# Attention with its steps in pairs, in all four head groups: transposes of two steps, then scores of two steps

## The chip, the cores and the metric

The kernel runs on one core of a Trainium2 chip (trn2). The metric is the device time of one execution in microseconds (us). TensorE (PE) does the matmuls and the transposes, and its weight loads (PEld) are recorded apart from them; VectorE (DVE) and ScalarE (ACT) do the elementwise work, GpSimd (POOL) a few powers and accumulating transfers, SyncE (SP) issues most transfers. Every engine takes its instructions in the order of its program and waits at semaphores.

## What is computed

One layer: a sparse attention mixer and a SwiGLU, each behind an RMS norm, for 512 tokens of width 2048. With 512 tokens each query may see all blocks of keys that lie before it, so the selected and the window branch both become causal attention, with keys and values of their own.

```python
h = rms_norm(x, norm_mix_g)
proj = h @ w_in                                   # 16 heads of queries, 6 x 4 groups of keys and values
o_cmp = softmax(q k_cmp) v_cmp                    # compressed blocks
o_sel = softmax(q k_sel, causal) v_sel            # branch b = 0
o_win = softmax(q k_win, causal) v_win            # branch b = 1
x = x + (g0 * o_cmp + g1 * o_sel + g2 * o_win) @ w_out
h = rms_norm(x, norm_ffn_g)
x = x + (silu(h @ w_gate) * (h @ w_up)) @ w_down
```

## The kernel before

Each engine has its own hand-written program in the kernel; there is no planner. Numbers in float32 are split into a high and a low part, and a product is three matmuls (`mm3`, L1674 is the line of every matmul in the traces): high by high, high by low, low by high. The weights come in units of 128 x 1024 elements: ScalarE copies the high part (`split`, L616), VectorE subtracts to get the low part (L1019).

**Groups and steps.** The attention runs in four groups of four heads. A group has 32 steps: for each head h, two branches b, and in each four tiles of queries, t = 0 to 3. Step i has t = i % 4, and its scores span t + 1 tiles of 128 keys. What is done for a step:

- TensorE, `scores(i)`: three matmuls into bank 2 + i % 2, 128 (t + 1) columns wide; for t = 0 both branches are done at once, so that step 4, 12, 20 and 28 have none of their own.
- VectorE, `maximum(i)` (L1321): mask, row maximum, copy to the probability buffer `pbuf[i % 2]`. There are two such buffers.
- ScalarE, `probs(i)` (L768): exp with sum, in place.
- VectorE, `weigh(i)` (L1329, L1331, L1336): reciprocal of the sum, times the gate; it gives `p_ready`.
- TensorE, transposes of the step's t + 1 tiles (L1996) into bank 4 + i % 2.
- ScalarE and VectorE, `pt_part(i)`: high part `pth` (L616) and low part `ptl` (L1344) of the transposed tiles. There is one such buffer for a block of four steps. The ScalarE copy of the first step of a block waits until the values matmuls of the block before have read it (`pv_done`).
- TensorE, `values(m)`: 12 matmuls, or 13 with the compressed branch, for block m of four steps, at step 4m + 5.

**Filler.** Between steps TensorE does matmuls that don't belong to the running softmax: in the first three groups the projections of the next group (`FILL_P`), in the last group the first three quarters of the output product (`FILL_A`). The lists give the half units ahead of each step's transposes; one takes 12 matmuls of 512 columns in the first groups, 24 of 256 in the last. From step 5 on, each step with values (5, 9, ... 29) has none, and in the first groups the other steps have one; in the last group they have two up to step 25.

```python
FILL_P = [[4, 5, 6], [7], [8], [9], [10], [], [11], [12], [13], [], [14], [15], [16], [], [17], [18],
          [19], [], [20], [21], [22], [], [23], [24], [25], [], [26], [27], [28], [], [29], [30]]
```

**What else rides along.** VectorE and ScalarE prepare weight units and move projections out of PSUM (`part_out`) after certain steps, by lists that follow from the filler. ScalarE waits for the filler's half unit that it copies or whose ring place it needs. For the next group's keys TensorE sums squares (`keys_sums` at `KSUM_AT`) and broadcasts the inverse roots over the partitions (`keys_bcast` at `KB_AT` and `KB2_AT`), and VectorE scales the keys with them (L1160, `keys_norm`). `compressed_thrice` (L1297) forms the weights of the compressed branch for the next head at steps 7, 15 and 23. In the last group ScalarE stages finished output columns and VectorE adds them (L1252).

**The order of a step.** TensorE: values if due, filler, transposes(i), scores(i + 2), then the next group's sums if due. VectorE: weigh(i - 1), low part of i - 2, maximum(i), what rides along. ScalarE: exp(i), high part of i - 1, what rides along.

## Time and profile before

| | |
|---|---|
| time, median of 3 runs | 2195.71 us (2193.26 to 2196.3) |
| the profiled execution's own time | 2192.59 us |
| its span, first to last instruction | 2190.6 us |
| TensorE busy, matmuls | 2176.8 us, 99% |
| VectorE busy | 1557.3 us, 71% |
| ScalarE busy | 1038.0 us, 47% |
| mean granted clock of TensorE | 0.997 |

The attention of the four groups begins at 266, 408, 549 and 691 us and each takes 110 us, the last 159 us. The time between them is the head of a group, dense with filler. Behind 852 us come the rest of the output product and the SwiGLU, which the change doesn't touch.

Rows of the timeline begin with the start and the duration in us. Matmuls are pipelined: one starts while the one before still drains, and the distance of starts tells what each takes from the engine. x4 says that four instructions of one form are merged. Square brackets give the idle time of the engine before and what ended it.

### The profile page before, as it was taken

How to read it: one execution, taken by the hardware profiler on the slowest of the kernel's cores; microseconds unless marked ns; L12 is line 12 of the kernel's file. 1: busy time of each engine (PE TensorE's matmuls, PEld its weight loads, DVE VectorE, ACT ScalarE, POOL GpSimd, SP SyncE). 2: the span in 40 equal slices, each digit the busy share in tenths (PEclk: the TensorE clock that was granted, in tenths of full speed). 3: DMA queues.
4: the chain of work that ended last, by engine and by line, in shares of the span. 5: the costliest groups of instructions: out<-in, count | busy, mean ns of one | idle time of the engine just before them, and what ended most of it. 6: DMA issues, size and time to landing. Idle time of an engine off the chain costs nothing.

```text
span 2190.6 us, 30130 instructions
## 1 busy us (share of the span) xinstructions
PE 2176.8 (99%) x11377; PEld 1867.0 (85%) x11377; DVE 1557.3 (71%) x2261; ACT 1038.0 (47%) x1482; POOL 101.1 (5%) x115
## 2 busy tenths in 40 slices
PE   9999999999999999999999999999999999999999
PEld 7898988989889998788888888888888888888887
DVE  6333466575666554798777777777877898989898
ACT  5332345343444333864445445445444565555553
POOL 1000000000001000100000000000000000000000
PEclk9999999999999999999999999999999999999999
DMA  5342212212214222644655555455465677666545
GB/s 177 116 116 87 78 59 59 68 49 67 60 59 145 68 68 81 208 164 122 179 162 161 154 165 178 120 163 178 131 175 163 185 225 237 192 192 197 174 143 164
DMA packets 209071, 300.49 MB, mean 137 GB/s; under 512 B 16588, under 2 KB 116209, under 8 KB 207521
## 3 DMA queue, kind: packets, MB, share of 16 engines
q1 hardware_dynamic: 197522, 255.40, 35.8%
q0 software_dynamic: 11408, 43.20, 9.5%
q8 instruction: 90, 1.47, 0.3%
q14 instruction: 51, 0.42, 0.1%
HBM read 235.35 MB, written 28.57 MB: 120 GB/s over the span
## 4 chain that ended last, share of the span: by engine, by line
PE 95%; DVE 2%; ACT 1%; issue 1%; DMA 0%; POOL 0%; SPq 0%; DVEq 0%; ACTq 0%
PE ps L1674 92%; PE ps L1996 1%; PE ps L2066 1%; DVE wl L1019 0%; DVE hTl L1019 0%; ACT wh L616 0%; DMA x_rows<-in_x_dram 0%; DVE x_rows L1051 0%; ACT left_val L865 0%; PE ps L1986 0%; PE ps L2031 0%; DVE ptl L1344 0%; DVE pbuf L1321 0%; ACT pbuf L768 0%; ACT sq L900 0%
## 5 line engine op out<-in xcount | busy, mean ns | idle before, releaser
L616 ACT ACTIVATE wh<-g 128x1024 fp32r<-128x1024 f32 x462 | 489.7, 1061 | 574.4 <-PE ps L1674 433.4
L1019 DVE TENSOR_TENSOR wl<-g,wh 128x1024 fp32r<-128x1024 f32 x462 | 564.5, 1222 | 225.2 <-PE ps L1674 217.4
L1674 PE MATMUL ps<-wh,left_hi 128*128 128x512 f32 x1232 | 481.7, 391 | 0.8 <-DVE wl L1019 0.5
L1674 PE MATMUL ps<-wh,left_lo 128*128 128x512 f32 x1232 | 479.7, 389 | 0.0
L1674 PE MATMUL ps<-wl,left_hi 128*128 128x512 f32 x1232 | 479.3, 389 | 0.0
L1674 PEld LDWEIGHTS ps<-wh,left_hi 128*128 128x128 f32 x1232 | 231.3, 188 | 49.3 <-issue 1.4
L1674 PEld LDWEIGHTS ps<-wh,left_lo 128*128 128x128 f32 x1232 | 231.3, 188 | 48.4
L1674 PEld LDWEIGHTS ps<-wl,left_hi 128*128 128x128 f32 x1232 | 231.4, 188 | 47.2
L1674 PE MATMUL ps<-wh,down_hi 128*128 128x512 f32 x616 | 239.8, 389 | 0.0
L1674 PE MATMUL ps<-wh,down_lo 128*128 128x512 f32 x616 | 239.7, 389 | 0.0
L1674 PE MATMUL ps<-wl,down_hi 128*128 128x512 f32 x616 | 239.6, 389 | 0.0
L1019 DVE TENSOR_TENSOR wl<-raw,wh 128x1024 fp32r<-128x1024 f32 x122 | 148.9, 1222 | 122.0 <-ACT wh L616 119.4
L1674 PE MATMUL ps<-hTh,wh 128*128 128x512 f32 (+1 forms) x560 | 215.4, 385 | 1.7 <-DVE wl L1019 1.0
L1674 PE MATMUL ps<-hTh,wl 128*128 128x512 f32 (+1 forms) x560 | 212.1, 379 | 0.0
L1674 PE MATMUL ps<-hTl,wh 128*128 128x512 f32 (+1 forms) x560 | 211.6, 378 | 0.0
L1674 PE MATMUL ps<-wh,hTh 128*128 128x256 f32 (+1 forms) x704 | 210.1, 298 | 0.7 <-DVE hTl L1019 0.3
L1674 PE MATMUL ps<-wl,hTh 128*128 128x256 f32 (+1 forms) x704 | 207.8, 295 | 0.0
L1674 PE MATMUL ps<-wh,hTl 128*128 128x256 f32 (+1 forms) x704 | 207.7, 295 | 0.0
L616 ACT ACTIVATE wh<-raw 128x1024 fp32r<-128x1024 f32 x122 | 128.8, 1059 | 125.5 <-PE ps L1674 106.2
L1674 PEld LDWEIGHTS ps<-wh,hTh 128*128 128x128 f32 x704 | 136.6, 194 | 6.0 <-issue 3.5
L1674 PEld LDWEIGHTS ps<-wh,hTl 128*128 128x128 f32 x704 | 136.6, 194 | 2.5
L1674 PEld LDWEIGHTS ps<-wl,hTh 128*128 128x128 f32 x704 | 136.7, 194 | 2.4
(214 smaller groups left out, 2985.5 us busy)
## 6 DMA issues: line engine op xcount, KB each, us to landing
g<-in_ffn_w_gate_dram SPq DMA_DIRECT2D x176, 256.0 KB, 3.1
g<-in_ffn_w_up_dram SPq DMA_DIRECT2D x176, 256.0 KB, 4.2
g<-in_ffn_w_down_dram SPq DMA_DIRECT2D x176, 256.0 KB, 4.9
raw<-in_nsa_w_in_dram SPq DMA_DIRECT2D x164, 256.0 KB, 3.0
g<-g POOLq DMA_DIRECT2D x66, 512.0 KB, 4.9
down_val<-m_scratch SPq DMA_DIRECT2D x77, 256.0 KB, 4.7
raw<-in_nsa_w_out_dram SPq DMA_DIRECT2D x64, 256.0 KB, 3.1
m_scratch<-work SPq DMA_DIRECT2D x22, 384.0 KB, 2.9
```

Source lines behind the costliest of these rows:

```text
L616: return nc.scalar.activation(dst, src, ACT.Copy)
L1019: nc.vector.tensor_tensor(dst, src, hi.bitcast(f32), ALU.subtract).then_inc(done, 1)
L1674: return nc.tensor.matmul(out_, a, b, start=start, stop=stop, skip_group_check=True)
L1996: last = nc.tensor.transpose(bank(4 + i % 2)[:, ks], pbuf[:, i % 2, ks], ident[:, :])
L2066: last = nc.tensor.transpose(bank(2 * spare + k)[:, tt * P:(tt + 1) * P], src, ident[:, :])
```

## The change

The flag `paired(g)` is true for all groups. TensorE treats the steps in pairs: at an even step i it does the transposes of i and of i + 1 and then the scores of i + 2 and of i + 3; at an odd step it does only values and filler. The sums and broadcasts for the next group come ahead of the transposes of their step instead of behind the scores, and two of their steps are moved to even numbers. On VectorE the weigh of an even step (i - 1, for odd i between 3 and 31) comes behind the maximum of the next step instead of ahead of its low part. `keys_bcast` makes one matmul of 512 columns instead of four of 128. The lists of the filler and ScalarE's program stay as they were.

```diff
--- before.py
+++ after.py
@@ -139,7 +139,7 @@
     + [[42], [43], [], [], [44], [45]]
 TAIL_A, END_A = [46], 47
 
-KSUM_AT, KB_AT, KB2_AT, QSUM_AT, KSPLIT_AT = 13, 17, 19, 26, STEPS - 2
+KSUM_AT, KB_AT, KB2_AT, QSUM_AT, KSPLIT_AT = 14, 18, 20, 26, STEPS - 2
 
 
 assert S // SEL_BLOCK <= N_SELECT and WINDOW >= S
@@ -354,6 +354,9 @@
                 self.local, self.per, self.i = 0, 0, 0
 
 
+
+        def paired(g):
+            return True
 
         WARM = 14
         H_BANKS = [0, 1, 2, 3, 4, 5, 6, 7, 2, 3, 4, 5, 6, 7, 2, 3]
@@ -1350,7 +1353,8 @@
                     for q in range(3, OWN // 2):
                         first_out(q)
                 for i in range(1, STEPS + 2):
-                    if i <= STEPS:
+                    weigh_last = paired(g) and 2 < i < STEPS and i % 2
+                    if i <= STEPS and not weigh_last:
                         weigh(i - 1)
                     if i % 8 == 2:
                         wait(dve, ptc_hi, i // 8 + 1, REP, g)
@@ -1360,6 +1364,8 @@
                         pt_part(i - 2)
                     if i < STEPS:
                         maximum(i)
+                    if weigh_last:
+                        weigh(i - 1)
                     if i == 1:
                         compressed_weigh()
                         splits(ended(HEAD_FILL))
@@ -1844,9 +1850,8 @@
                 wait(pe, kdiag_ready, 1, 1, p)
                 if b:
                     wait(pe, k_norm, 1, 2, p)
-                for t in range(TT):
-                    last = mm(bank(0)[:, t * P:(t + 1) * P], inv128[:, :], diag[:, b * TT + t, :], True, True)
-                last.then_inc(kb_done, 1)
+                mm(bank(0), inv128[:, :], diag[:, b * TT:(b + 1) * TT, :].rearrange("p j c -> p (j c)"), True, True)\
+                    .then_inc(kb_done, 1)
 
             def queries_sums(p, h0):
 
@@ -1965,51 +1970,63 @@
                 compressed_scores()
                 for w in HEAD_FILL[0 if last_group else 2:]:
                     filler(w)
+                def compressed_transposes(h):
+                    wait(pe, pc_ready, h + 1, REP, g)
+                    if h:
+                        wait(pe, ptc_ready, h, REP, g)
+                    if not last_group and h == 2:
+                        wait(pe, k_den, 1, 1, g + 1)
+                    if not last_group and h == 3:
+                        wait(pe, k_norm, 2, 2, g + 1)
+                    for tt in range(TT):
+                        last = nc.tensor.transpose(bank(0)[0:3 * CPAD, tt * P:(tt + 1) * P],
+                                                   pc3[:, tt, :, :].rearrange("p r c -> p (r c)"), ident[:, :])
+                    last.then_inc(trc_done, 1)
+
+                def next_group_sums(i):
+                    if i in (KSUM_AT, KB_AT, QSUM_AT):
+                        wait(pe, ptc_ready, i // 8 + 1, REP, g)
+                    if i == KSUM_AT:
+                        keys_sums(g + 1)
+                    if i == KB_AT:
+                        keys_bcast(g + 1, 0)
+                    if i == KB2_AT:
+                        keys_bcast(g + 1, 1)
+                    if i == QSUM_AT:
+                        queries_sums(g + 1, 0)
+
+                def transposes(i):
+                    wait(pe, p_ready, i + 1, STEPS, g)
+                    if i == 1:
+                        wait(pe, q_den, 2, 2, g)
+                    if i >= 2:
+                        wait(pe, pt_lo, i - 1, STEPS, g)
+                    for k in range(i % TT + 1):
+                        ks = slice(k * P, (k + 1) * P)
+                        last = nc.tensor.transpose(bank(4 + i % 2)[:, ks], pbuf[:, i % 2, ks], ident[:, :])
+                    last.then_inc(tr_done, 1)
+
                 for i in range(STEPS):
-                    t = i % TT
-                    if i > TT and t == 1:
+                    if i > TT and i % TT == 1:
                         values(i // TT - 1)
                     for w in fill[i]:
                         filler(w)
                     if last_group and i == STEPS - 1:
                         filler(tail[0], (0,))
                     if i % 8 == 0:
-                        h = i // 8
-                        wait(pe, pc_ready, h + 1, REP, g)
-                        if h:
-                            wait(pe, ptc_ready, h, REP, g)
-                        if not last_group and h == 2:
-                            wait(pe, k_den, 1, 1, g + 1)
-                        if not last_group and h == 3:
-                            wait(pe, k_norm, 2, 2, g + 1)
-                        for tt in range(TT):
-                            last = nc.tensor.transpose(bank(0)[0:3 * CPAD, tt * P:(tt + 1) * P],
-                                                       pc3[:, tt, :, :].rearrange("p r c -> p (r c)"), ident[:, :])
-                        last.then_inc(trc_done, 1)
-                    wait(pe, p_ready, i + 1, STEPS, g)
-                    if i == 1:
-                        wait(pe, q_den, 2, 2, g)
-                    if i >= 2:
-                        wait(pe, pt_lo, i - 1, STEPS, g)
-                    for k in range(t + 1):
-                        ks = slice(k * P, (k + 1) * P)
-                        last = nc.tensor.transpose(bank(4 + i % 2)[:, ks], pbuf[:, i % 2, ks], ident[:, :])
-                    last.then_inc(tr_done, 1)
-                    if i + 2 < STEPS:
-                        scores(i + 2)
-                    if last_group:
-                        continue
-                    if i == KSUM_AT:
-                        wait(pe, ptc_ready, KSUM_AT // 8 + 1, REP, g)
-                        keys_sums(g + 1)
-                    if i == KB_AT:
-                        wait(pe, ptc_ready, KB_AT // 8 + 1, REP, g)
-                        keys_bcast(g + 1, 0)
-                    if i == KB2_AT:
-                        keys_bcast(g + 1, 1)
-                    if i == QSUM_AT:
-                        wait(pe, ptc_ready, QSUM_AT // 8 + 1, REP, g)
-                        queries_sums(g + 1, 0)
+                        compressed_transposes(i // 8)
+                    if not last_group:
+                        next_group_sums(i)
+                    if not paired(g):
+                        transposes(i)
+                        if i + 2 < STEPS:
+                            scores(i + 2)
+                    elif i % 2 == 0:
+                        transposes(i)
+                        transposes(i + 1)
+                        if i + 2 < STEPS:
+                            scores(i + 2)
+                            scores(i + 3)
                 for w in tail:
                     filler(w, (1,) if last_group else (0, 1))
                 values(2 * REP - 1)
```

## Rows read from the trace of the kernel before

**Rows 1.** The page, part 1: busy us, share of the span, instructions

```profile
PE 2176.8 (99%) x11377; PEld 1867.0 (85%) x11377; DVE 1557.3 (71%) x2261; ACT 1038.0 (47%) x1482; POOL 101.1 (5%) x115
```

**Rows 2.** Windows: stretch, length, busy us by engine, clock, DMA; first group's steps

```profile
266.10:375.80 109.70, 109.52 (x609) 94.55 (x608) 75.14 (x226) 52.51 (x127) 3.27 (x2) 1.00 0.20 58
```

**Rows 3.** Timeline of TensorE: start, us, instruction; transposes of step 15 and scores

```profile
318.63 0.60 PE L1996 MATMUL ps<-ident,pbuf 128*128 128x128 f32 x4
318.99 0.36 PE L1674 MATMUL ps<-kh,qh 128*128 128x256 f32 x1
319.19 0.28 PE L1674 MATMUL ps<-kl,qh 128*128 128x256 f32 x1
```

**Rows 4.** A broadcast in the timeline; plain fp32 of 512 columns in the groups by form

```profile
333.58 1.05 PE L1674 MATMUL ps<-sq,inv 128*128 128x128 f32 x8
...
L1674 PE MATMUL ps<-gain_line,ones 1*128 1x512 f32 x8 | 7.2, 1069 | 2.7 <-DMA gain_line<-in_norm_mix_g_dram 2.7
```

**Rows 5.** Timeline of TensorE: last of values(0), filler, transposes(6), transposes(7)

```profile
282.49 0.28 PE L1674 MATMUL ps<-pth,vl 128*128 128x128 f32 x1
...
283.55 0.40 PE L1674 MATMUL ps<-hTh,wh 128*128 128x512 f32 x1
...
286.31 0.49 PE L1996 MATMUL ps<-ident,pbuf 128*128 128x128 f32 x3
...
289.74 0.49 PE L1996 MATMUL ps<-ident,pbuf 128*128 128x128 f32 x3
```

**Rows 6.** Timeline of ScalarE: pth(4), exp(6), pth(5), exp(7)

```profile
282.87 0.28 ACT L616 ACTIVATE pth<-ps 128x128 fp32r<-128x128 f32 x1 [3.41 <-PE ps L1674]
284.04 0.62 ACT L768 ACTIVATE pbuf<-pbuf,nb 128x384 f32<-128x384 f32 x1 [0.89 <-DVE nb L1321]
...
284.65 0.36 ACT L616 ACTIVATE pth<-ps 128x256 fp32r<-128x256 f32 x1
286.68 0.72 ACT L768 ACTIVATE pbuf<-pbuf,nb 128x512 f32<-128x512 f32 x1 [1.66 <-DVE nb L1321]
```

**Rows 7.** Timeline of VectorE: maximum(6), weigh(6), ptl(5), maximum(7), compressed, weigh(7)

```profile
283.38 0.61 DVE L1321 CUSTOM_DVE_ANT_0 pbuf<-ps,causal,nrq 128x384 f32<-128x384 f32 x1
...
285.16 0.48 DVE L1336 TENSOR_SCALAR pbuf<-pbuf,wgt,gates_g 128x384 f32<-128x384 f32 x1
285.56 0.42 DVE L1344 TENSOR_TENSOR ptl<-ps,pth 128x256 fp32r<-128x256 f32 x1
285.89 0.74 DVE L1321 CUSTOM_DVE_ANT_0 pbuf<-ps,causal,nrq 128x512 f32<-128x512 f32 x1
...
286.56 0.56 DVE L1297 TENSOR_TENSOR pc<-pc,csum 128x384 f32<-128x384 f32 x1
...
287.92 0.55 DVE L1336 TENSOR_SCALAR pbuf<-pbuf,wgt,gates_g 128x512 f32<-128x512 f32 x1
```

**Rows 8.** Timelines of ScalarE and VectorE: pth(28) and the end of weigh(31)

```profile
368.67 0.28 ACT L616 ACTIVATE pth<-ps 128x128 fp32r<-128x128 f32 x1 [3.39 <-PE ps L1674]
...
373.73 0.55 DVE L1336 TENSOR_SCALAR pbuf<-pbuf,wgt,gates_g 128x512 f32<-128x512 f32 x1
```

**Rows 9.** Timeline of VectorE: the second scaling of the next group's keys

```profile
334.74 0.69 DVE L1160 TENSOR_TENSOR kst<-kst,ps 128x512 f32<-128x512 f32 x1 [1.94 <-PE ps L1674]
```

**Rows 10.** Timelines in the last group: pth(4) and the end of weigh(7)

```profile
713.66 0.28 ACT L616 ACTIVATE pth<-ps 128x128 fp32r<-128x128 f32 x1 [6.42 <-PE ps L1674]
...
720.87 0.55 DVE L1336 TENSOR_SCALAR pbuf<-pbuf,wgt,gates_g 128x512 f32<-128x512 f32 x1
```

**Rows 11.** Timeline of TensorE in the last group: transposes(26)

```profile
832.59 0.55 PE L1996 MATMUL ps<-ident,pbuf 128*128 128x128 f32 x3 [1.36 <-DVE pbuf L1336]
```

**Rows 12.** Timeline of TensorE at a group's head; windows there and near 830

```profile
391.93 0.26 PE L1674 MATMUL ps<-kcg,ql 128*128 128x32 f32 x1
...
392.70:396.10 3.40, 3.40 (x18) 3.40 (x17) 3.23 (x8) 0.00 (x0) 0.00 (x0) 0.51 0.00 0
829.50:832.90 3.40, 2.04 (x19) 1.84 (x17) 2.89 (x7) 1.27 (x4) 0.00 (x0) 1.00 0.05 11
```

## What the change will do to the time

> **What bounds the kernel now.** I read the busy line of the page first: TensorE works for 99% of the span [rows 1]. The window over the attention of the first group says the same for that stage alone: 109.52 of 109.70 us, while VectorE works 75.14 and ScalarE 52.51 [rows 2]. So nothing is to be had from other engines unless they let TensorE wait, and anything that makes it wait is paid in full. Next I read TensorE's timeline where transposes meet matmuls, to learn what an alternation costs, and then the timelines of all three engines over steps 4 to 7, where a block of values lies. There the reader is to see two things: how late each probability tile is ready before TensorE wants it, and how few instructions can run side by side on ScalarE and VectorE.
>
> **What the change moves.** TensorE's order per step was: values (at every fourth step), filler, transposes(i), scores(i+2). It becomes, for an even i: filler of i, transposes(i), transposes(i+1), scores(i+2), scores(i+3), and then the filler of i+1 (with values before it where i+1 is 5, 9, ... 29). No work is dropped. It runs in all four groups.
>
> *Gain from fewer alternations.* Four transposes start at 318.63 and the second matmul behind them starts at 319.19, 0.56 us later [rows 3]. Five instructions at the 0.11 us that separates transposes make 0.55. An alternation thus costs about 0.01 us here, although the first matmul's own record is longer (0.36 against 0.28): it starts early and seems to wait inside the engine. There are 64 alternations fewer: 0.6 us. The upper bound, if the 0.08 us of record length were real, is 64 x 0.08 = 5 us. I take 0.5, since the distance of starts is what the next instruction feels.
>
> *The single 512-column broadcast* replaces four of 128 columns, in eight calls. Eight records take 1.05 us now; the nearest record of 512 plain fp32 columns is 1.07 us, two to a call, in the cold start [rows 4]. Bounds: from 2 x 0.23 us as for the one-pass 512-column matmuls to 2 x 1.07, so -5 to +9 us in all. The same columns are streamed, so I take 0.
>
> *Loss from the moved transposes, worked out for steps 4 to 7.* Two probability buffers exist, so maximum(6) can't start before transposes(4) are copied out, nor maximum(7) before those of 5. ScalarE's copy of step 4 waits besides for the values matmuls, because it overwrites pth: it starts at 282.87, after 3.41 us of waiting, when the last values matmul ends at 282.77 [rows 5, 6]. From there both engines take turns, in their program order. ScalarE: pth(4), exp(6), pth(5), exp(7). VectorE: ptl(4), maximum(6), then weigh(6), ptl(5), maximum(7), compressed tile, weigh(7) [rows 7]. weigh(7) ends at 288.47, so the chain from the end of values, call it V, some 0.05 us ahead of the copy, is 5.6 us. TensorE wants that tile at 289.74 [rows 5], 1.3 us later: the chain is hidden because between V and transposes(7) lie transposes(5), scores(7), filler(6), transposes(6), scores(8) and filler(7), 6.9 us.
>
> After the change transposes(5), scores(6) and scores(7) lie ahead of V, scores(8) and filler(7) behind transposes(7). What remains as cover is filler(6), 283.55 to 286.31 = 2.76 us, and three transposes of 0.11 us: 3.1 us [rows 5]. The chain gets shorter by less than one weigh, since weigh(6) moves behind maximum(7) and partly beside exp(7), but the compressed tile moves into it: pth(5) ends 285.01, ptl(5) 285.4, maximum(7) 286.1, weigh(6) 287.0, compressed 287.4, weigh(7) 288.25. V to weigh(7) is 5.4 us. TensorE stands for 5.4 + 0.4 (wait to end of the first transpose) - 3.1 - 0.1 = 2.6 us. Before, it did not stand at all there.
>
> The same sum for the other six such places of the group, each from the start of the first step's copy to the end of the last weigh (the last of them 368.67 to 374.28, again 5.6 [rows 8]): steps 8 to 11, with a split (1.06 on ScalarE, 1.22 on VectorE) in the chain, 2.7; 12 to 15, where the sums of squares now run ahead of transposes(14) and add about 1.95 us of cover, 1.2; 16 to 19, split and key scaling in the chain, one broadcast as cover, 2.5; 20 to 23, 2.6; 24 to 27, sums as cover, 1.2; 28 to 31, no compressed tile, 2.3. Sum 15.1 us.
>
> *Places without values* (pair to pair over two fillers, 5.5 us, and scores) fit more nearly. What is new there is that a split or copy of an odd step on ScalarE waits for that step's filler, which now comes after the transposes, and that the next exp is queued behind it. I get 0.4, 0.5, 0.3 and 0.4 us for pairs 2, 14, 22 and 26, none for 6 and 10. At pair 18 VectorE's second key scaling stands ahead of weigh(21) and waits for the broadcast, which is now directly ahead of transposes(20). It already waits 1.94 us today [rows 9]. After it come 0.69 of scaling and some 0.85 of weigh, less what two transposes cover: 1.6 us. Sum 3.2 us. The present small waits (about 0.6 us a group) go. Per group 15.1 + 3.2 - 0.6 = 17.7, for the first three groups 53 us.
>
> *The last group.* Its value places have two halves of filler (5.8 us) behind V, but the chain is longer, since the staging copies, their additions and a split stand in it: from the copy at 713.66 to the end of weigh(7) at 721.42 [rows 10] and 0.05 before it, 7.8 us, and VectorE works through nearly without a break, so reordering saves nothing. Pause 7.8 + 0.4 - 5.8 - 0.4 = 2.0 us at three places; at two more with a head's output in the chain 2.6. At 24 to 27 only one half of filler is left: 8.4 us of chain against 3.0, so 5.4; pair 26, again one half with a split behind it, 3.3; 28 to 31, 2.1. Sum 6.0 + 5.2 + 10.8 = 22.0. Off go today's waits there, those ahead of transposes, the longest of 1.36 idle [rows 11], 2.9 with their late starts, six of 0.3 for staged banks and 0.4 at the end: 5.1. Net 17 us.
>
> *TensorE's clock.* In 392.7 to 396.1 the granted clock was 0.51, the lower level of 1.2 GHz, after a run of matmuls with only 32 or 64 columns, of which one row stands for all 32; in 829.5 to 832.9, with 1.36 us idle, it stayed at 1.00 [rows 12]. Pauses of 2 us and more with only transposes between them stream as little as the former. A fall costs as here: sixteen 256-column matmuls 0.21 apart instead of 0.12, 1.5 us. With 28 pauses I take five falls as visible, 7 us; bounds 0 and 28 x 1.5 = 42. The Trainium skill, "TensorE: Matmul & The Clock Gate", section "HAM oscillation — how this bites in real kernels", says that a wait between bursts of matmuls which is long enough puts the array back to the lower clock, burst after burst. No pause in this trace has done so; by that rule without exception the 7 us would be the 42 of the second rival, and without any such pause 0.
>
> **The sum.** 53 + 17 - 0.5 + 7 = 76.5 us on the profiled execution, which took 2192.6 (span 2190.6): 2269. That execution is 3.1 us under the median of 2195.71; on the median I forecast 2272 us.
>
> **The rivals.**
> 1. *The pauses are half as long.* My chains assume that no instruction on ScalarE and VectorE overlaps another beyond what the rows show, and that the other places resemble steps 4 to 7. Against: both queues are in order and the steps in the chain depend on each other. 35 + 4 gives 2235. Chance 0.12.
> 2. *The clock falls after nearly every pause.* 70 + 42 gives 2308. For: long stretches with little streaming. Against: 1.00 at 829.5 [rows 12]. Chance 0.08.
> 3. *Faster.* The alternation really costs 0.08 us or more and the saved column sits in the records' length, while the chains stay covered. It decides for the change only if TensorE still has 5.4 us of work between the end of values and transposes(7), where I count 3.1. It would give 2195.7 - 5 = 2191. Against: the distance of starts in [rows 3]. Chance 0.03.
> 4. *It doesn't do what it says*, the order on TensorE being bound elsewhere, so that pairs wait for nothing new: 2196. Chance 0.04.
>
> **How the numbers follow.** My own case has 0.73 and reaches from 2248 (no falls, chains 0.5 us shorter) to 2296 (fifteen falls). Rival 1 is next, so the range goes down to 2238 and leaves 2308 out. About 0.2%, 4.4 us, is what a measurement of this kernel can tell from no change. Slower 0.93, same 0.04, faster 0.03.
>
> **What would show it.** Right: TensorE idle before transposes 6, 10, 14, ... of each group, released by the weigh of VectorE, 1 to 2.7 us together per pair, most in the pair after values; the pth copy of a first step still released by the values matmul; busy time of TensorE unchanged, its share near 96%; granted clock under 1.00 in a few stretches of the attention. The stages after it keep their length. Wrong: an unchanged share of 99%, or the idle time at heads of groups instead. The forecast falls if cover and chain in steps 4 to 7 don't differ by some 2.5 us.

## The result and the profile after

The kernel with the change takes 2283.72 us (median of 4, 2281.27 to 2287.33), the kernel before beside it 2194.49 us (2192.74 to 2196.3): a ratio of 1.0407, 95% interval 1.0394 to 1.042. It is 4% slower, 89.2 us. The profiled execution of the changed kernel was the longest of its four, 2287.33 us at a span of 2285.4, so on the spans of the two profiles the difference is 94.8 us; both figures are used below, each where it says so. The measured time lies 11.7 us above the forecast of 2272.

The page's busy line and its chain that ended last, of the changed kernel:

```profile
PE 2213.0 (97%) x11329; PEld 1886.0 (83%) x11329; DVE 1560.8 (68%) x2261; ACT 1037.6 (45%) x1482; POOL 101.1 (4%) x115
PE 88%; DVE 6%; ACT 4%; issue 1%; DMA 0%; POOL 0%; SPq 0%; ACTq 0%; DVEq 0%
```

TensorE runs the same work in 97% of a longer span, where it had 99% [rows 1], and a tenth of the chain is now VectorE and ScalarE, where it was 3% before. Its busy time also grew, by 36 us, which the prediction had said would stay: some 26 us of that is work done at a lower clock (worked out below), and the other 10 go with the waits, since the instruction behind a wait has a longer record. The windows over the steps of attention of the four groups (length, busy us of TensorE, its weight loads, VectorE, ScalarE and GpSimd, granted clock, DMA):

```profile
266.40:397.90 131.50, 117.22 (x585) 97.58 (x584) 74.68 (x225) 51.01 (x126) 3.27 (x2) 0.94 0.17 49
433.30:565.10 131.80, 117.53 (x585) 97.65 (x584) 74.70 (x225) 51.01 (x126) 3.27 (x2) 0.94 0.17 49
600.50:729.00 128.50, 114.22 (x585) 95.09 (x584) 74.72 (x225) 51.01 (x126) 3.27 (x2) 0.96 0.16 50
763.40:939.10 175.70, 156.68 (x1198) 150.88 (x1197) 87.57 (x232) 60.68 (x140) 0.00 (x0) 0.98 0.20 63
```

They answer to [rows 2], where the first group took 109.70 us at full clock with TensorE busy for 109.52. The first three hold 24 records fewer than before: 12 because a broadcast is two records instead of eight, and 12 because the filler of step 31 (2.8 us) now lies behind the last transposes. The last holds 36 fewer, all of them filler of step 31. TensorE's waits from 266 to 940 us (total us, times, longest):

```profile
PE ps L2006 <- DVE pbuf L1339: 55.8, 59, 3.1
PE ps L1680 <- ACT vst L619: 3.0, 3, 1.0
PE ps L1680 <- ACT kst L619: 3.0, 3, 1.0
```

Before, the transposes waited for VectorE's weigh 2.2 us in all, twice. Now it is 59 times. The other six waits are all in the last group, in front of filler whose result ScalarE stages. The place that the prediction worked out, steps 4 to 7 of the first group, in the timelines of ScalarE, VectorE and TensorE:

```profile
284.76 0.28 ACT L619 ACTIVATE pth<-ps 128x128 fp32r<-128x128 f32 x1 [5.56 <-PE ps L1680]
285.93 0.62 ACT L771 ACTIVATE pbuf<-pbuf,nb 128x384 f32<-128x384 f32 x1 [0.89 <-DVE nb L1324]
286.55 0.36 ACT L619 ACTIVATE pth<-ps 128x256 fp32r<-128x256 f32 x1
288.07 0.72 ACT L771 ACTIVATE pbuf<-pbuf,nb 128x512 f32<-128x512 f32 x1 [1.16 <-DVE nb L1324]
```
```profile
285.28 0.61 DVE L1324 CUSTOM_DVE_ANT_0 pbuf<-ps,causal,nrq 128x384 f32<-128x384 f32 x1
286.94 0.42 DVE L1347 TENSOR_TENSOR ptl<-ps,pth 128x256 fp32r<-128x256 f32 x1 [1.05 <-ACT pth L619]
287.28 0.74 DVE L1324 CUSTOM_DVE_ANT_0 pbuf<-ps,causal,nrq 128x512 f32<-128x512 f32 x1
288.33 0.48 DVE L1339 TENSOR_SCALAR pbuf<-pbuf,wgt,gates_g 128x384 f32<-128x384 f32 x1
288.73 0.55 DVE L1300 TENSOR_TENSOR pc<-pc,csum 128x384 f32<-128x384 f32 x1
289.58 0.55 DVE L1339 TENSOR_SCALAR pbuf<-pbuf,wgt,gates_g 128x512 f32<-128x512 f32 x1
```
```profile
287.06 0.39 PE L1680 MATMUL ps<-hTh,wl 128*128 128x512 f32 x1
288.87 0.55 PE L2006 MATMUL ps<-ident,pbuf 128*128 128x128 f32 x3 [1.42 <-DVE pbuf L1339]
290.18 0.66 PE L2006 MATMUL ps<-ident,pbuf 128*128 128x128 f32 x4 [0.76 <-DVE pbuf L1339]
```

These are [rows 5 to 7] once more, now with two gaps on TensorE. The copy of step 4 still waits for the last matmul of values. From there to the end of weigh(7), at 290.13, it is 5.4 us, in the order maximum(6), ptl(5), maximum(7), weigh(6), compressed tile, weigh(7).

### The profile page after: what moved, and what is told of

Read it like the earlier page. It is cut to its first block, busy times and chain, and to the rows that moved or that the text cites. A ratio compares the mean times of both kernels' runs of the same rounds, so it can differ in the third digit from the quotient of the medians.

```text
span 2285.4 us, 30034 instructions
## 1 busy us (share of the span) xinstructions
PE 2213.0 (97%) x11329; PEld 1886.0 (83%) x11329; DVE 1560.8 (68%) x2261; ACT 1037.6 (45%) x1482; POOL 101.1 (4%) x115
## 3 DMA queue, kind: packets, MB, share of 16 engines
q8 instruction: 90, 1.47, 0.3%
## 4 chain that ended last, share of the span: by engine, by line
PE 88%; DVE 6%; ACT 4%; issue 1%; DMA 0%; POOL 0%; SPq 0%; ACTq 0%; DVEq 0%
PE ps L1680 85%; PE ps L2006 2%; DVE pbuf L1339 1%; ACT wh L619 1%; DVE pbuf L1324 1%; PE ps L2083 1%; ACT pbuf L771 1%; DVE wl L1022 1%; DVE ptl L1347 1%; DVE wgt L1334 0%; ACT pth L619 0%; DVE x_rows L1255 0%; DMA x_rows<-in_x_dram 0%; DVE hTl L1022 0%; DVE x_rows L1054 0%
## 5 line engine op out<-in xcount | busy, mean ns | idle before, releaser
L1680 PE MATMUL ps<-hTh,wh 128*128 128x512 f32 (+1 forms) x560 | 220.7, 394 | 1.2 <-DVE wl L1022 1.0
L1347 DVE TENSOR_TENSOR ptl<-ps,pth 128x128 fp32r<-128x128 f32 (+2 forms) x160 | 64.8, 421 | 150.2 <-ACT pth L619 131.1
```

Of the source, the lines that this page charges most:

```text
L1347: last_ = nc.vector.tensor_tensor(dst, src, hi.bitcast(f32), ALU.subtract)
L1680: return nc.tensor.matmul(out_, a, b, start=start, stop=stop, skip_group_check=True)
```

## The experiments

A pause below is taken at the transposes alone. It is the time by which the end of a step's first transpose lies further behind the end of the instruction before it than the 0.11 us that it takes unwaited; it is longer than the idle time in brackets, by 0.24 us a wait on average in the first three groups (18.3 us of pauses against 14.3 idle, 17 pauses). By that measure the changed kernel pauses 18.2 to 18.4 us in each of the first three groups.

**Which groups pay: e1, e2, e3.** Each kernel is the changed one with one line of `paired` other than `return True`; the single broadcast and the order of the sums stay in all three.

```diff
 def paired(g):
-    return True
+    return g < LAST        # e1_first_three
+    return g == LAST       # e2_last_only
+    return False           # e3_unpaired
```

> Pairs in the first three groups only, the last group as before. Theory (pauses where a block of values lies, counted place by place): the last group's pauses, 18 us net, and its share of the clock falls, about 3 us, go: 2263 us. Rival (the pauses come from the sums and broadcasts that were moved ahead of the transposes, which the last group doesn't have): the time stays within 3 us of the 2284 of the changed kernel, since the last group would have cost nothing.

> Pairs in the last group only. Theory: 18 us of net pauses there and some 3 us of clock falls: 2215 us. Rival (moved sums and broadcasts): within 4 us of the kernel before.

> No group in pairs; what is left of the change is the sums and broadcasts ahead of the transposes, with their steps moved, and the single 512-column broadcast. Theory: nothing measurable, 2194 +- 3 us, a broadcast taking two records of 0.43 us in place of eight of 0.11. Rival (moved sums): 10 us or more slower, because VectorE's scaling of the keys waits for them in front of a weigh.

Measured: e1 2260.64 us, ratio 1.0296 (1.028 to 1.0312); e2 2215.19, 1.0093 (1.0078 to 1.0109); e3 2193.11 over 11 runs, 0.9992 (0.9983 to 1.0001), each beside 2195.38 for the kernel before. Windows over the first group's steps and the last group's, first of e1 and then of e2:

```profile
266.10:397.90 131.80, 117.52 (x585) 97.63 (x584) 74.70 (x225) 51.03 (x126) 3.27 (x2) 0.94 0.17 49
766.80:925.90 159.10, 156.47 (x1234) 151.72 (x1233) 87.32 (x232) 60.93 (x139) 0.00 (x0) 1.00 0.22 69
```
```profile
269.30:378.80 109.50, 109.34 (x597) 93.55 (x596) 75.36 (x226) 52.60 (x127) 3.27 (x2) 1.00 0.20 59
691.70:866.00 174.30, 155.27 (x1198) 149.76 (x1197) 87.60 (x232) 60.68 (x139) 0.00 (x0) 0.99 0.20 63
```

Each group is long exactly where it is paired, and the groups hardly act on each other: 65.3 us for the first three and 19.8 for the last make 85.1 of the 88.3 that the whole change costs against the same kernel before. The 3.2 us between them are within the spread of e1's own runs (2258.55 to 2268.8). The rest of the diff, the single broadcast and the shifted sums, is worth nothing that e3 can tell: its interval holds 1.

**The granted clock: e4.** The changed kernel, with matmuls put into the pauses of the first three groups and nothing moved. They multiply values already there, into the two banks that the transposes are about to overwrite, so their results are not used.

```diff
+ pad = not last_group and i >= 6 and i % 4 == 2
+ if pad and i not in (14, 26):
+     wait(pe, pt_lo, i - 1, STEPS, g)
+     for _ in range(4 if i == 18 else 5):
+         mm(bank(4), vh[:, 0, 0:P], vh[:, 0:2, :]...)
  transposes(i)
+ if pad:
+     wait(pe, pt_lo, i, STEPS, g)
+     for _ in range(3):
+         mm(bank(5), vh[:, 0, 0:P], vh[:, 0:2, :]...)
  transposes(i + 1)
```

> The changed kernel with extra 512-column matmuls (their results are overwritten at once) in the pauses of the first three groups: four or five ahead of transposes 6, 10, 18, 22 and 30, three between the two sets of transposes at those and at 14 and 26. 45 extra matmuls of 0.23 us a group, 31 us in all. Theory (the clock falls come from pauses in which nothing streams, and cost about 16 us in these groups beside the waits): the pads fill idle time, the clock stays at 1.00 in the first three groups, 2268 us or somewhat more where a pad overruns its pause. Rival (the falls come from the transposes lying together, or from heads of groups): clock as in the changed kernel, 2284 us or more. Second rival (TensorE doesn't stand idle, the chain is elsewhere): the full 31 us on top, 2315 us.

Measured: 2268.64 us (2263.34 to 2270.18), ratio 1.033 (1.0314 to 1.0346). With 45 matmuls more per group it is 15.1 us faster than the changed kernel. Windows of e4 over the steps of the first and the third group, and its timeline at steps 6 and 7:

```profile
267.80:391.90 124.10, 119.53 (x630) 99.00 (x629) 74.70 (x225) 51.13 (x126) 3.27 (x2) 1.00 0.18 52
585.20:709.30 124.10, 119.51 (x630) 98.95 (x629) 74.72 (x225) 51.10 (x126) 3.27 (x2) 1.00 0.17 52
```
```profile
288.73 1.29 PE L1680 MATMUL ps<-vh 128*128 128x512 f32 x5
290.31 0.55 PE L2006 MATMUL ps<-ident,pbuf 128*128 128x128 f32 x3 [0.29 <-DVE pbuf L1339]
290.61 0.95 PE L1680 MATMUL ps<-vh 128*128 128x512 f32 x3
```

The transposes come no earlier, but the clock stays at 1.00 and every group takes the same 124.1 us instead of 131.5, 131.8 and 128.5. This splits the loss in two: 15.1 us are the clock in the steps of the first three groups, and 73.3 (2268.64 against 2195.38) are what is left, the waits and the falls of the clock at heads and in the last group. The windows give the price of a fall: 7.4, 7.7 and 4.4 us off the three groups for five, five and three low stretches, 1.5 us each. The low stretches can be seen in windows of the changed kernel at the place above:

```profile
287.60:291.00 3.40, 1.36 (x10) 1.13 (x11) 2.39 (x9) 2.25 (x4) 0.00 (x0) 0.99 0.00 0
291.00:294.40 3.40, 3.40 (x12) 2.82 (x11) 3.02 (x9) 1.03 (x4) 0.00 (x0) 0.50 0.00 0
294.40:297.80 3.40, 3.40 (x17) 2.76 (x16) 1.37 (x8) 0.60 (x2) 0.00 (x0) 1.00 0.51 154
```

TensorE was busy 1.36 of 3.4 us around the two pauses; in the 3.4 us behind them it was granted 0.50, the level of 1.2 GHz, and got through 12 matmuls, against 17 in the next 3.4 us.

**The order on VectorE: e7.** The changed kernel with weigh(6) ahead of maximum(7) again, as before.

```diff
- weigh_last = paired(g) and 2 < i < STEPS and i % 2
+ weigh_last = False
```

> The changed kernel with VectorE's old order: weigh of the even step ahead of the low part and maximum of the odd one, in all steps. Theory (weigh sits in the chain of the pair; behind the maximum it runs beside exp): the chain gets 0.2 us longer where a compressed tile follows and 0.5 where not, 28 places, 8 us with the places without values: 2293 us. Rival (the order on VectorE is of no account): 2284 +- 3 us.

Measured: 2300.25 us, ratio 1.0488 (1.0469 to 1.0507), 16.5 us slower than the changed kernel. Of e7, on VectorE and on TensorE:

```profile
286.99 0.48 DVE L1339 TENSOR_SCALAR pbuf<-pbuf,wgt,gates_g 128x384 f32<-128x384 f32 x1
```
```profile
290.34 0.65 PE L2006 MATMUL ps<-ident,pbuf 128*128 128x128 f32 x4 [2.27 <-DVE pbuf L1339]
```

weigh(6) comes 1.3 us earlier and the pause moves from in front of transposes(6) to in front of transposes(7): 0.37 + 2.49 instead of 1.64 + 0.98. A pair pays for its later tile, so the first one's earliness is worth nothing; only the sum counts, and it grew by 0.24 us here and by 0.5 at steps 30 and 31. Over the first three groups the pauses grew by 8.6 us, in the last by 0.6. The stretches at the lower clock last 75.1 us in sum against 68.3 in the changed kernel, two more of 3.4 us, some 3 us at the 1.5 that each costs. Together that is 12 us, and the two profiled executions differ by 11.1 (2298.41 against 2287.33). The medians differ by 16.5, twice the 8 us that I had expected, since the changed kernel's profiled execution was its slowest; over all runs the mean clock is 0.979 to 0.983 here against 0.985 to 0.988, so more of that difference is clock. The part of the change that reorders VectorE thus does what it is for; within the pairs it is the part that pays.

**What starts the chain: e5.** The values matmuls from one step earlier, ahead of the filler of the even step, so that the whole filler of two steps lies behind them.

```diff
- if i > TT and i % TT == 1:
+ if i and i % TT == 0:
      values(i // TT - 1)
```

> The changed kernel with each block of values one step earlier: ahead of the filler of step 4m+4, hence ahead of that pair's transposes instead of behind its scores. Theory (ScalarE's copy of a block's first step waits for the values matmuls, and the chain of both engines starts only there): the chain starts at transposes(4m+4), and the scores (1.2 us) become cover, of which 0.4 is lost because maximum waits for its scores; about 1.1 us less pause at each of 7 places in a group, about 1.3 less between the other pairs, which the values now cover: 32 us off with the last group, and some 8 us fewer clock falls: 2244 us, range 2230 to 2262. Rival (the two probability buffers alone set the chain, the values don't matter): 2284 +- 4 us.

Measured: 2239.78 us, ratio 1.0222 (1.0192 to 1.0252), 43.9 us faster than the changed kernel. The pauses of a group go from 18.3 to 11.8 us, 19 us for three groups; those in front of the last group's transposes from 15.5 to 11.6, and the waits of 1.0 us for staged copies in the list above are gone from its list. Against that, one block of values in each of the first three groups now waits 1.26 us for a low part. In the profiled execution no low stretch is left in the steps of the first three groups, which gives the 15 us of e4 as well. That isn't so in every run: the fourth took 2249.99 us at a mean clock of 0.991, where the other three took 2238.95 to 2239.93 at 0.997. ScalarE and TensorE of e5 at the same place:

```profile
282.62 0.28 ACT L619 ACTIVATE pth<-ps 128x128 fp32r<-128x128 f32 x1 [3.39 <-PE ps L2006]
```
```profile
287.23 0.55 PE L2006 MATMUL ps<-ident,pbuf 128*128 128x128 f32 x3 [0.47 <-DVE pbuf L1339]
288.54 0.66 PE L2006 MATMUL ps<-ident,pbuf 128*128 128x128 f32 x4 [0.77 <-DVE pbuf L1339]
```

The copy of step 4 is released by its own transposes now, and the pauses at the seven places with values fall from 15.4 to 10.1 us a group. This shows that the values matmul ahead of the copy was what the prediction took it for: the start of the chain that is longer than its cover. It also shows the limit of that: with the start freed, two thirds of the pauses stay, because the chain from the transposes themselves is still longer than the cover.

**More cover by moving filler: e8 and e6.** FILL_P gives every step 0 to 3 half units of filler. In both kernels the step without filler is 4m+4 instead of 4m+5 in the first three groups, so that the transposes of 4m+5 and of 4m+6 have two half units of filler between them instead of one. e8 is the changed kernel with that, e6 is e5 with that.

```diff
- ... [10], [], [11], [12], [13], [], [14], [15], [16], [], [17], [18],
+ ... [], [10], [11], [12], [], [13], [14], [15], [], [16], [17], [18],
```

> The changed kernel with only the filler moved (first three groups): two half units after each block of values, one between the other pairs; values where the change has them. Theory (each kind of pair needs its own cover, about 5.5 us after the values, 6 without them): the pauses behind values (15 us a group) vanish and as much comes up between the other pairs, 2 to 2.7 us at each of seven places: 2280 us, range 2268 to 2292. Rival (only the places with values are short of cover): 45 us and the clock falls go, 2225 us or less.

> As the run with early values, and in the first three groups the step without filler is 4m+4 instead of 4m+5, so that both kinds of pairs have about 7 us of matmuls between their transposes. Theory (cover against chain): the pauses of the first three groups fall to 0.5 us a place at most, except the one at the second broadcast (1.7), and the clock stays up there: 20 us under the run with early values for waits and about 8 for the clock, 2214 us, range 2203 to 2230. Rival (a pair costs by itself, wherever the filler stands): within 6 us of the run with early values.

Measured: e8 2304.8 us, 1.0505 (1.0486 to 1.0524); e6 2238.8, 1.02 (1.0182 to 1.0219). Both missed what I expected, by 25 us each, and lie outside the ranges that I had given. The time of e6 is the one that its rival named, that a pair costs by itself; e12 below decides against that rival. ScalarE of e6 between steps 8 and 10:

```profile
300.34 1.06 ACT L619 ACTIVATE wh<-raw 128x1024 fp32r<-128x1024 f32 x1 [1.16 <-PE ps L1680]
301.31 0.71 ACT L771 ACTIVATE pbuf<-pbuf,nb 128x512 f32<-128x512 f32 x1
```

The split of an odd step's filler stands on ScalarE ahead of the next exp and waits for that filler, whose release is now later: an exp that feeds the next transposes is held by work that nobody waits for. The pauses of e8 rose from 18.3 to 22 or 23 us a group, with new ones in front of transposes 4 and 5 (1.20 + 2.41), 12 and 13, and 24 and 25; those of e6 fell only from 11.8 to 8.9. And in e6 the granted clock fell again, twice each in the steps of the first and the third group and at two heads, which took most of the 9 us that shorter pauses gave.

**Readers of rides: e9 and e12.** e9 is e5 with the five VectorE parts that prepare the next group's keys and queries (denominators, scaled diagonals and the two scalings) issued one step later each: four of them now stand behind the weigh of an odd step instead of ahead of it, and the fifth, the scaled diagonals, comes to stand ahead of weigh(17). e12 is e6 with that and with everything that an odd step's filler leaves on ScalarE and VectorE (splits, copies out) put off to the next even step.

```diff
- if j == KSUM_AT - 1:   # keys_den; the same for KB_AT - 1, KB2_AT - 1, QSUM_AT - 1
+ if j == KSUM_AT:
- if j == KSUM_AT:       # keys_diag
+ if j == KSUM_AT + 1:
+ def even_steps(of, fill, j):                        # e12 only
+     if j == STEPS - 1: return of(fill, j)
+     return [] if j % 2 else (of(fill, j - 1) if j else []) + of(fill, j)
```

> The run with early values, with VectorE reading the sums and broadcasts for the next group's keys and queries one step later, hence behind the weigh of the odd step instead of ahead of it. Theory (the moved sums cost where VectorE waits for TensorE's sum or broadcast and the weigh is queued behind that): of the pauses of that run those at transposes 15 (0.93 us), 21 (1.67) and 27 (0.93) go and that at 19 (1.35) falls by 0.7, 4 us a group: 2228 us, range 2222 to 2236. Rival (these pauses are the chain of maximum, exp and weigh itself): 2240 +- 3 us.

> The run with early values and moved filler, with the later readings and with all splits and copies of odd steps put behind the even step after them (first three groups), so that ScalarE never waits for a filler ahead of an exp. Theory (what is left there are VectorE's waits for sums, 4 us a group, and ScalarE's waits for the odd step's filler, 3 us a group): the pauses of the first three groups fall from 9 to 2 or 3 us each, 2238.8 - 19 = 2220 us, a few us less if the clock stays up, range 2208 to 2230. Rival (a pair is short of cover in principle): 2238 +- 4 us.

Measured: e9 2225.04 us, 1.0137 (1.0122 to 1.0152), with 7.7 us of pauses a group; e12 2213.45, 1.0084 (1.0069 to 1.0098), with 1.1. The pauses at 15, 21 and 27 that e5 still had went with the moved readers (0.93 to 0, 1.67 to 0, 0.93 to 0.07), those behind odd fillers with the moved splits. Of e12, the one wait that is left in front of a group's transposes, and its cause on VectorE, the scaled diagonals in front of weigh(17); and, in the second group, the longest wait of all, in front of a filler:

```profile
324.94 0.44 PE L2011 MATMUL ps<-ident,pbuf 128*128 128x128 f32 x2 [0.79 <-DVE pbuf L1344]
```
```profile
322.52 1.66 DVE L1162 TENSOR_SCALAR sq<-ident,krr 128x128 f32<-128x128 f32 x8
```
```profile
495.81 0.47 PE L1685 MATMUL ps<-hTh,wh 128*128 128x512 f32 x1 [1.32 <-DVE ql L1027]
```

So the pauses in front of transposes can be taken away nearly in full without giving up the pairs, and what pairs are worth by themselves can be read. (The last group of e12 is still paired as in e5, with 11.7 us of pauses.) A whole second group, from its first transposes to the third group's, of e12 and then of the unpaired e11 below:

```profile
413.40:557.50 144.10, 141.25 (x846) 124.45 (x845) 91.12 (x264) 60.93 (x143) 5.89 (x3) 1.00 0.21 59
```
```profile
407.00:547.50 140.50, 140.32 (x846) 123.96 (x844) 91.33 (x264) 61.38 (x143) 5.81 (x3) 1.00 0.21 61
```

The same 846 instructions take 3.6 us longer in pairs. 2.7 us of that are idle (144.10 - 141.25 against 140.50 - 140.32), in five waits, behind each of which TensorE needs another 0.2 us or so until its matmuls overlap again. That leaves nothing that 16 alternations fewer could have gained, within the few tenths to which the 0.2 is known. Blocks without a wait tell it more closely. From the first transpose to the first instruction behind the scores, steps 8 and 9 of the first group take 1.56 us as a pair in e12 and 0.64 + 0.95 = 1.59 apart in e11; steps 6 and 7 take 1.47 as a pair and 0.68 + 0.79 = 1.47 apart; steps 18 and 19 take 1.12 as a pair and 0.25 + 0.79 = 1.04 apart.

**A version without pairs: e10 and e11.** e10 is e3 with two of the half units of the last group that lay in steps 23 and 24 given to steps 26 and 28, where its transposes waited [rows 11]. e11 is e10 with a half unit of filler put between the two halves of the compressed scores, at the heads where the clock fell [rows 12].

```diff
- for c in range(6) ... + [[42], [43], [], [], [44], [45]]
+ for c in range(5) ... + [[36, 37], [38], [39], [], [40, 41], [42], [43], [], [44], [45]]
- compressed_scores()
+ compressed_scores(range(8))                 # e11, first three groups
+ filler(HEAD_FILL[2])
+ compressed_scores(range(8, 16))
```

> No group in pairs, and in the last group two half units of filler moved from steps 23 to 25 to steps 26 and 28, where the kernel before waits 1.6 and 1.1 us for the weigh. Theory: TensorE is idle for want of filler there, the waits go: 2190.3 us, 0.2 to 0.25% under the kernel before with the 0.1% of the unpaired run. Rival (the chain of VectorE and ScalarE is delayed as much): as the unpaired run, 2193.

> As the run before it, and at the head of each of the first three groups a half unit of filler stands between the two halves of the compressed scores, matmuls of 32 and 64 columns. Theory (the clock falls at heads because nothing but such small matmuls runs there for a while): a fall of 1.6 us at one of three heads goes: 2189 us. Rival (it falls for another reason): as the run before it, within 1 us.

Measured: e10 2192.09 us over 11 runs, 0.9988 (0.9979 to 0.9997); e11 2189.48, 2188.37 to 2190.06 over 9 runs, 0.9975 (0.9966 to 0.9985), beside 2194.99 for the kernel before. e11 is the fastest kernel of this case, 0.25% ahead of before. One more run of e11 took 5633.18 us; it isn't among the nine, and nothing here explains it. Expected were 2190.3 and 2189 us. By its median e10 is only 1.0 us under e3, and the two intervals overlap; its profiled execution, with low stretches as long in sum as those of e3's, is 2.6 us shorter (2191.14 against 2193.7), near the 2.85 us of pauses that went. Of e10, transposes(26) and transposes(28):

```profile
828.27 0.49 PE L2006 MATMUL ps<-ident,pbuf 128*128 128x128 f32 x3
836.53 0.27 PE L2006 MATMUL ps<-ident,pbuf 128*128 128x128 f32 x1
```

Neither has idle time in front any more. In e11 no low stretch is left at the heads of the first three groups; the last group's head, which was not split, still has one of 10.2 us from 664.7. In e10 one of three heads had one (532.7 us). One profile each would not show much, since e5's has none there either without the split; but the mean clock of e11's nine runs is 0.998 in seven and 0.997 in two, and of e10's eleven 0.997 in six and 0.996 in five.

## Why the prediction was right, step by step

**The chain against its cover: right.** It was worked out at 5.4 us from V to weigh(7), with 2.6 us of pause. The rows of the changed kernel show 5.4 (284.76 to 290.13) and 1.64 + 0.98 = 2.62. The other value places of a group, predicted and measured: steps 8 to 11 2.7 and 2.8; 12 to 15 1.2 and 1.4; 16 to 19 2.5 and 2.3; 20 to 23 2.6 and 2.6; 24 to 27 1.2 and 1.2; 28 to 31 2.3 and 2.35. Sum 15.1 and 15.4. e5 shows that it is this chain: when its start is freed, the pauses at these places fall by 5.2 us a group.

**Places without values: right in sum, not one by one.** Pair 2 stands for what lies between the transposes of 2 and 3 and those of 4 and 5, and so on. Pair 2 0.4 and 0.74; pair 14 0.5 and nothing; pair 18 1.6 and 1.67; pair 22 0.3 and nothing; pair 26 0.4 and 0.56. Sum 3.2 and 3.0. At pair 18 it is the mechanism named, the second key scaling in front of a weigh:

```profile
350.03 1.02 PE L1680 MATMUL ps<-sq,inv 128*128 128x512 f32 x2
350.88 0.27 PE L2006 MATMUL ps<-ident,pbuf 128*128 128x128 f32 x1
352.61 0.44 PE L2006 MATMUL ps<-ident,pbuf 128*128 128x128 f32 x2 [1.45 <-DVE pbuf L1339]
```
```profile
351.15 0.69 DVE L1163 TENSOR_TENSOR kst<-kst,ps 128x512 f32<-128x512 f32 x1 [1.28 <-PE ps L1680]
352.14 0.41 DVE L1339 TENSOR_SCALAR pbuf<-pbuf,wgt,gates_g 128x256 f32<-128x256 f32 x1
```

**The single broadcast: right, at nothing.** The first of the rows above shows that it became two records with 0.85 us from their start to that of the next instruction, where eight records took 1.05 with their last one's drain [rows 4]. In e3, which keeps it, nothing of it can be measured.

**The last group: right in size (17 predicted, 18 measured), with a third of the waits elsewhere than I had said.** Its transposes pause 15.5 us in all, and another 7.5 us lie in front of staged filler, at six places of 1.24 where I had taken away six of 0.3; 23.0 in all against my 22.0, less some 5 that had been there before. Place by place the two kinds together are what I had: 2.0 at the three places with 2.0 predicted (0.80 + 1.24), 2.65 at the two with 2.6, 5.7 at steps 24 to 27 with 5.4, then 3.3 with 3.3 and 2.2 with 2.1; only 0.4 us at step 3 I didn't have. Rows of the changed kernel:

```profile
788.66 0.36 PE L1680 MATMUL ps<-wh,hTh 128*128 128x256 f32 x1 [1.01 <-ACT vst L619]
795.56 0.66 PE L2006 MATMUL ps<-ident,pbuf 128*128 128x128 f32 x4 [0.58 <-DVE pbuf L1339]
917.42 0.55 PE L2006 MATMUL ps<-ident,pbuf 128*128 128x128 f32 x3 [2.35 <-DVE pbuf L1339]
927.86 0.44 PE L2006 MATMUL ps<-ident,pbuf 128*128 128x128 f32 x2 [3.07 <-DVE pbuf L1339]
```

The first stands at one of the six: the filler's staging copy is itself queued on ScalarE inside the chain, so filler that I had counted as cover waited for it. The last group's loss of 19.8 us in e2 is these 18 and, in its profile, one low stretch more than before.

**Fewer alternations: right, too small to be found.** e12 against e11 leaves nothing for them: a pair starts 0.03 us earlier to 0.08 us later behind its block than two steps apart do, where I had 0.01 us for each alternation. The distance of starts was the view to trust, and the longer record of the first matmul behind transposes was not time.

**The clock: the term that was mis-sized.** I took five falls for 7 us. The trace shows 16 low stretches in the steps and 3 at heads, 68.3 us long in sum, where before had 2 at heads, 10.2 us long. Summed over the distances of starts in them, the time beyond what the same instructions take at full clock is 29.8 us, against 4.2 before, so some 26 us more. The price of one, 1.5 us, was right; their number was not. The windows of e4 agree: 19.5 us for the 13 in the steps of the first three groups of this execution, the slowest of four; by the medians e4 measured 15.1 there. The step that failed was "five falls as visible": I set [rows 12], a pause of 1.36 us at full clock, as the likelier pattern against the run of short matmuls that had brought a fall, though most of my pauses come in twos, with only three transposes between them (steps 6 and 7, 10 and 11, and so on). The second rival, a fall after nearly every pause, came true in part, 16 low stretches for 28 places; its 42 us were not reached.

By the spans: 69 us of waits (51 in the first three groups and 18 in the last) and 26 of clock, together the 94.8 measured. So the 69.5 us that I had for all but the clock were right, and the error is the clock. For the profiled execution, for which the sum was made, it is 18.3 us (94.8 against 76.5); the medians miss by 11.7 only because that execution, the one with 26 us of clock, was the slowest of its kernel. By the medians, with e4 between them, 15.1 us are the clock in the steps of the first three groups, where I had 7 for all falls, and the 73.3 that are left hold the waits and the other falls, where I had 69.5 for waits.

The Trainium skill, "TensorE: Matmul & The Clock Gate", section "HAM oscillation — how this bites in real kernels", describes the same loss, work done at the lower clock after each wait that comes between bursts. This case agrees in kind, but the waits here are short ones for another engine, none idle for more than 1.9 us in the first three groups, not long ones for a transfer.

Not settled is why a given pause brings a fall and another none. The length doesn't decide it: at steps 14 and 15 (1.4 us of pause) and 26 and 27 (1.2) there is one in each of the three groups, at steps 18 and 19 (2.3) in none. And of three groups with the same pauses to 0.2 us, the first two had five falls and the third had three, and runs of the same kernel differ by 6 us (2281.27 to 2287.33) with a mean clock of 0.988 to 0.985.

## What to carry to other kernels

Where TensorE is the bound and waits for nothing, as here, pairing the steps of a pipeline can take away the filler between two steps that hid the work of the other engines. Add up the in-order chain from the last thing that it waits for, add up what TensorE still has between the two, and the difference is the loss. Here that gave each place with values in the first three groups to 0.2 us; at the places without values it was up to 0.5 us off. Before moving filler to lengthen the cover, look at what each filler leaves behind on the other engines' queues, since it moves too and can hold the very instruction that is late (e6, e8). And count a pause twice: once for its length and once for the clock behind it, which matmuls of no use can keep up (e4), though it is better not to have the pause.

## What the runs showed of the hardware that was not expected

- Behind two waits of 1.4 and 0.8 us idle, with three transposes between them, the granted clock was 0.50 for 3.4 us; there 512-column matmuls start 0.42 us apart instead of 0.23. The same two waits brought no fall in the third group:

```profile
291.72 0.63 PE L1680 MATMUL ps<-hTh,wh 128*128 128x512 f32 x1
292.14 0.63 PE L1680 MATMUL ps<-hTl,wh 128*128 128x512 f32 x1
```

- Forty-five extra matmuls a group, put where TensorE stood idle, left the transposes where they were and made the kernel 15.1 us faster.
- A falling clock needs no idle engine: at a group's head it fell behind a run of 64- and 32-column matmuls, with TensorE busy for all of the 3.4 us [rows 12]. With one half unit of filler in the middle of that run, e11 had no fall at those heads and was 2.6 us shorter by the medians (2192.09 to 2189.48), 1.1 by the profiled executions.
